# Coefficients, gelu and diagonals of an expert pair ahead of the dense work of odd ticks

## The reference, cut to what matters

```python
def peer_ffn(h, w_q, sub_keys, u_tab, v_tab):
    ...
    expert = i1 * PEER_KEYS + i2
    gate = jax.nn.softmax(best_s, axis=-1)
    u_e = jnp.take(u_tab, expert, axis=0)
    v_e = jnp.take(v_tab, expert, axis=0)
    act = jax.nn.gelu(jnp.einsum('chkd,cd->chk', u_e, xc).astype(jnp.float32))
    return jnp.einsum('chk,chkd->cd', (gate * act).astype(v_e.dtype), v_e)

def reference(...):
    for l in range(DEPTH):
        ...
        x = x + peer_ffn(rmsnorm(x, norm_ffn_g[l]), peer_wq[l], peer_sub_keys[l], peer_u[l], peer_v[l])
    return rmsnorm(x, final_norm_g)
```

## Time and profile before

| | |
|---|---|
| time, median of 3 runs | 1727.95 us (1727.3 to 1729.12) |
| the profiled execution's own time | 1728.54 us |
| its span, first to last instruction | 1726.5 us |
| granted TensorE clock, mean | 0.99 of full |
| bytes moved by DMA | 680.38 MB, 394 GB/s over the span |
| experts' gathers | 512, 536.90 MB |
| busy share | PE 91%, PE weight load 55%, VectorE 70%, ScalarE 35%, GpSimd 34% |

### The profile page before, as it was taken

One profiled execution on the slowest core, in us unless ns is written; L12 is line 12 of the kernel. 1 busy time (PEld: TensorE's weight loads), 2 busy tenths in 40 slices (PEclk: granted clock), 3 DMA queues, 4 the chain that ended last, 5 costly groups with the idle time before them and its releaser, 6 DMA issues.

```text
span 1726.5 us, 19576 instructions
## 1 busy us (share of the span) xinstructions
PE 1579.6 (91%) x6594; PEld 957.9 (55%) x6594; DVE 1212.9 (70%) x3359; ACT 601.0 (35%) x1451; POOL 586.4 (34%) x527
## 2 busy tenths in 40 slices
PE   8999999998999999998999889999999997777776
PEld 7877866545557776644645557644655553322232
DVE  7731689985885767897556477898656677667665
ACT  4133341553344132255232242255323223222222
POOL 0000243443333323344334243344333344433331
PEclk9999999999999999999999999999999999999999
DMA  9637799999999999999999999999999999999996
GB/s 382 243 131 263 291 403 422 415 413 421 421 420 420 422 421 421 420 413 420 421 422 420 421 416 420 421 363 407 422 421 421 421 419 421 421 421 422 422 421 259
DMA packets 94579, 680.38 MB, mean 394 GB/s; under 512 B 10488, under 2 KB 10768, under 8 KB 12304
## 3 DMA queue, kind: packets, MB, share of 16 engines
q0 software_dynamic: 73728, 536.90, 75.2%
q1 hardware_dynamic: 20752, 142.24, 20.4%
HBM read 678.06 MB, written 1.05 MB: 393 GB/s over the span
## 4 chain that ended last, share of the span: by engine, by line
PE 48%; DMA 33%; DVE 11%; ACT 5%; issue 3%; POOL 0%; SPq 0%; DVEq 0%; ACTq 0%
DMA slots<-expert_rows,expert 32%; PE bank L855 21%; PE bank L412 9%; DVE slots L1780 5%; PE bank L590 4%; PE bank L843 3%; PE bank L840 3%; ACT diag L1308 1%; PE bank L457 1%; DMA ring<-w_blocks 1%; PE bank L475 1%; DVE sg L1347 1%; PE bank L678 1%; PE bank L490 1%; ACT L1321 1%
## 5 line engine op out<-in xcount | busy, mean ns | idle before, releaser
L855 PE MATMUL bank<-slots,diag 128*128 128x512 f32 x1916 | 904.0, 608 | 127.8 <-ACT diag L1308 125.4
L967 POOL DMA_INDIRECT slots<-expert_rows,expert x512 | 584.5, 1142 | 1115.1 <-PE bank L855 861.6
L1780 DVE CUSTOM_DVE_ANT_0 slots<-slots,htok 128x1024 f32<-128x1024 f32 x512 | 626.1, 1223 | 332.4 <-DMA slots<-expert_rows,expert 322.6
L855 PEld LDWEIGHTS bank<-slots,diag 128*128 128x128 f32 x1916 | 346.7, 192 | 541.1 <-issue 321.3
L1321 ACT ACTIVATE gel<-dot 128x2 f32<-128x2 f32 (+1 forms) x258 | 52.5, 204 | 671.9 <-DVE dot L1780 664.0
L412 PEld LDWEIGHTS bank<-hT,ring 128*128 128x128 f32 x1712 | 208.5, 193 | 50.5 <-issue 44.9
L1308 ACT ACTIVATE diag<-ident,coef 128x128 f32<-128x128 f32 x479 | 168.2, 395 | 186.2 <-DVE coef L1347 179.5
L412 PE MATMUL bank<-hT,ring 128*128 128x128 f32 x1712 | 209.8, 276 | 4.8 <-DMA ring<-w_blocks 3.9
L1347 DVE SCALAR_TENSOR_TENSOR coef<-gel,ginv,gexp 128x2 f32<-128x2 f32 (+1 forms) x258 | 54.6, 212 | 57.6 <-ACT gel L1321 49.2
L1321 ACT ACT_TABLE_LOAD x66 | 84.7, 1283 | 1.2
L1347 DVE SCALAR_TENSOR_TENSOR sg<-pad,prm,sg 128x128 f32<-128x128 f32 x240 | 71.4, 342 | 0.0
(11 more groups left out here) (315 smaller groups left out, 1543.2 us busy)
## 6 DMA issues: line engine op xcount, KB each, us to landing
ring<-w_blocks SPq DMA_DIRECT2D x98, 1024.0 KB
slots<-w_blocks SPq DMA_DIRECT2D x24, 1024.0 KB, 8.0
slots<-expert_rows,expert POOLq DMA_INDIRECT x512
kept<-w_blocks SPq DMA_DIRECT2D x4, 1024.0 KB, 11.4
keys<-w_blocks SPq DMA_DIRECT2D x2, 1024.0 KB, 10.8
prm<-small SPq DMA_DIRECT2D x2, 768.0 KB
x<-x_rows SPq DMA_DIRECT2D x2, 512.0 KB, 11.0
slots<-mem_rows SPq DMA_DIRECT2D x1, 1024.0 KB, 9.8
```

What stands on the lines that cost most here:

```text
L855: last = mm(bank[h][:, :], diag[:, i % DIAGS, :], slots[:, n % SLOTS, D + h * 512:D + (h + 1) * 512], start=m == 0, stop=n == end)
L967: nc.gpsimd.indirect_dma_start(slots[:, n % SLOTS, :], None, experts_d, bass.IndirectOffsetOnAxis(ap=idx[q % 2][:, k:k + 1], axis=0),).the ...
L1780: v.tensor_tensor_reduce(out=slots[:, s, 0:D], in0=slots[:, s, 0:D], in1=htok[:, ph % 2, :], scale=1.0, scalar=0.0, op0=ALU.mult, op1=ALU.add,
```

## The change

In odd ticks that have a pair, ACT now makes gelu first, then waits for the coefficients and makes both diagonals, and only then does the dense pieces of that tick. Nothing of the experts is left at the head of even ticks. VectorE does the route piece ahead of the dense pieces in every tick, and in odd ticks it waits for gelu and makes the coefficients ahead of the dense pieces and of an add of its own. For the last four experts, ACT makes the diagonal in the tick of its gelu. No instruction is added or taken away, and no buffer is changed.

```diff
@@ scalar engine
             for tick in range(LAST):
                 n = tick - G0
-                if 2 <= n <= SINGLE and n % 2 == 0:
-                    eng.wait_ge(coef_ready, n // 2)
-                    for k in (n - 2, n - 1):
+                if 0 <= n < SINGLE and n % 2:
+                    gelu(n - 1, 2)
+                    eng.wait_ge(coef_ready, n // 2 + 1)
+                    for k in (n - 1, n):
                         if TAKER[k] == "tensor":
                             diagonal(k)
-                if SINGLE < n <= NG:
-                    eng.wait_ge(coef_ready, SINGLE // 2 + n - SINGLE)
-                    diagonal(n - 1)
                 go_on(strands, tick)
-                if 0 <= n < SINGLE and n % 2:
-                    gelu(n - 1, 2)
                 if SINGLE <= n < NG:
                     gelu(n, 1)
+                    eng.wait_ge(coef_ready, SINGLE // 2 + n - SINGLE + 1)
+                    diagonal(n)
@@ vector engine
-                go_on(strands, tick)
                 go_on(route, tick)
-                if 2 <= n <= NG and n % 2 == 0 and TAKER[n - 1] == "vector":
-                    add_slot(n - 1)
                 if 0 <= n < SINGLE and n % 2:
                     eng.wait_ge(gelu_ready, n // 2 + 1)
                     coefficients(n - 1, 2)
+                go_on(strands, tick)
+                if 2 <= n <= NG and n % 2 == 0 and TAKER[n - 1] == "vector":
+                    add_slot(n - 1)
```

## The result

| | before | after |
|---|---|---|
| median of the runs | 1727.84 us (6 runs, 1726.03 to 1729.12) | 1735.97 us (6 runs, 1732.67 to 1738.99) |
| ratio, 95% interval | | 1.0048 (1.0037 to 1.0059) |
| profiled execution, its span | 1728.54, 1726.5 us | 1738.99, 1737.0 us |

The change makes the kernel slower by 0.0048 x 1728 = 8.3 us (6.4 to 10.2), where no change was forecast (1728.4), and its median lies just above the range that the forecast gave, 1723.0 to 1735.0. The profiled execution of after is the slowest of its six, 3 us above their median, so its losses sum to more than 8.3.

The account below looks back on a forecast made before the run. DMA engines were taken as the bound. Start -1.0, stage 3 +0.8, stages 1 and 2 +0.3 each made +0.4 us, a profiled 1728.9; with runs' median 0.6 lower, the forecast was 1728.4 us, range 1723.0 to 1735.0.

Parts of the forecast that it names:

- What bounds the kernel: From the first gathers on, DMA engines set the end; full at 421 GB/s, idle 12 us in all, the largest possible gain.
- Part 1: Coefficients ahead of VectorE's dense pieces: slots freed earlier, gaining 1.0 us per VectorE-bound stretch, bounds 0 and 2.5 us.
- Part 2: VectorE's new wait for gelu in odd ticks: 1.8 us lost in stage 3, the same taken for stages 1 and 2.
- +0.3 each: Net loss in us summed for stages 1 and 2, in place of +0.8, as filled slots hide part.
- their engines hardly idled: Reason for the smaller loss in stages 1 and 2: DMA engines idled only 1.3 and 0.9 us there.
- Part 3: ACT's dense pieces behind gelu and diagonals in odd ticks: price 0; 6 us a stage if the cover were gone.
- five gathers ahead: Cover in full DMA stretches: about five gathers issued ahead of the dot, 12 us of work, outlast PE's 6 us loss.
- Part 4: Start, end and rest: first coefficients some 4 us earlier, part of the 240 us gap goes; gain 1.0 us, bounds 0 and 1.9.
- A: Rival, slower: VectorE's new waits count in full in attention ticks of stages 1 to 3; 5.4 us, about 1733.5; chance 0.20.
- The test set for A: In the windows 1120 to 1200 us, DMA idle time exceeds 10 us; near 7 would confirm the forecast.
- B: Rival, faster: earlier release fills DMA gaps in stage 3 (4.8 us) and at the start (1.0); about 1722.5 us; chance 0.20.
- C: Rival, slower: PE's stalls for held-back ACT evacuations aren't covered, 6 us a stage, 18 us in all: 1746 us; chance 0.05.

Follow-up runs that it names:

- VectorE's lateness at `BEGIN` + 81: Kernel before plus a needless 2600-element VectorE reduction (2.85 us), behind the coefficients, in tick `BEGIN` + 81 of each attention stage: 1728.48 us, ratio 0.9999.
- all but the 15 ticks and the start: Changed kernel with the old order up to n = 10 and in ticks `BEGIN` + 33, 37, 41, 45, 47 of stages 1 to 3: 1727.99 us, ratio 1.0008.
- the 15 ticks alone: Kernel before with the new order only in ticks `BEGIN` + 33, 37, 41, 45, 47 of stages 1 to 3: 1733.06 us, ratio 1.0039.
- 2.85 us of pure lateness: Two kernels: before plus a needless 2600-element VectorE reduction in tick `BEGIN` + 41 per attention stage, behind coefficients (1732.85 us) or ahead of dense pieces (1733.38 us).
- half of it: Kernel before plus a needless 1300-element VectorE reduction (1.50 us), behind the coefficients of tick `BEGIN` + 41 in each attention stage: 1731.49 us, ratio 1.0014.

## Why the prediction was wrong

**What bounds the kernel**: right. The loss is idle time of the DMA engines (11.8 us in the windows for 10.5 of span), most of it in the three attention stretches that the prediction named. That full stretches hide what happens in them holds for VectorE's lateness at `BEGIN` + 81, where 2.85 us cost nothing, but not for every stall: 200 to 240 us was full before and lost 1.7 us.

**Part 1**, coefficients ahead: a gain of 1.0 us in each VectorE-bound stretch was taken. No run shows it. With the new order in all but the 15 ticks and the start nothing is gained, and with it in the 15 ticks alone 6.7 us are lost. The rows of the profile behave as the part says (a diagonal 0.2 to 0.3 us behind its coefficients, 1162.36 against 1162.10), but an earlier diagonal is worth nothing if PE then stands at a later instruction in its list.

**Part 2**, the wait for gelu: three of the four waits came near. VectorE waits 1.69 us at tick 397, where 0.75 was the scan's wait, so 0.9 more (forecast 1.1); 1.28 at tick 401 against 0.17, 1.1 more (forecast 1.6); 0.84 at tick 407 against 1.92, 1.1 less (forecast 0.9 less). But at tick 405, where the prediction had "gelu in time", it waits 1.78 us:

```profile
1176.48 0.25 DVE L1345 SCALAR_TENSOR_TENSOR coef<-gel,ginv,gexp 128x2 f32<-128x2 f32 x1 [1.78 <-ACT gel L1321]
1182.33 0.22 DVE L1345 SCALAR_TENSOR_TENSOR coef<-gel,ginv,gexp 128x2 f32<-128x2 f32 x1 [0.84 <-ACT gel L1321]
```

In sum 2.7 us for stage 3, where 1.8 was said. The wait at 405 comes back from PE: ACT's attention functions ahead of that gelu waited 2.19 us for products of PE that stood behind the late transposes. In the kernel of the fifteen ticks, where PE's stall was shorter, tick 405 has no such wait. The total over the kernel went from 49.2 to 54.5 us:

```profile
DVE coef L1345 <- ACT gel L1321: 54.5, 73, 5.0
```

**The step that failed is the one in the sum** that turned this lateness into time: "+0.3 each" in stages 1 and 2, "part is hidden by filled slots", and 1.0 us set against it. In tick + 41 there is hardly such a cover: 2.85 us of pure lateness cost 2.2 us a stage and half of it 0.8; and the gain of Part 1 that was set against it, 1.0 us a stage, no run shows. The prediction counted how many slots stood filled ahead of VectorE's dot; what the DMA engines need is empty slots, and these are made by PE's adds. PE works its list in order, so the adds stand behind line 508 or behind their own diagonal, whichever is late. In stages 1 and 2 I took "their engines hardly idled" for a cover; it meant that they had more to lose (4.8 and 2.7 us in the windows). A second term stood at nothing without a word: PE's clock. Behind the stall it fell to the lower level in all three stages, and that kept GpSimd waiting 3.2 us longer in stage 3 than at the full clock.

**Part 3**, evacuations behind gelu and diagonals: price 0, "PE needs an odd tick's evacuation in the very next tick only in the memory attention". Wrong in the start: at tick 107 PE waits for the scores' evacuation, 4.28 us against 1.17. ACT's order alone costs 5.0 us (2.9 to 7.1). Its cover in full stretches, "five gathers ahead", held in after, where they stay at 421 GB/s, but not with ACT's order alone: there 2.59 us of waiting for an evacuation at 509.17 left 1.7 us of gaps. In after PE comes to this place otherwise; it waits 5.66 us at 503.62 for VectorE's `htok` and loses nothing. Why the same order loses there in one kernel and not in the other isn't shown; the price of 0 was luck in part.

**Part 4**, the start: first coefficients at 204.54 (forecast 205.5, before 209.46), so the cause was right and the gain of 1.0 wasn't: the windows from 200 to 260 lose 1.4 us against before. The gap that the gain was to be taken from is mostly chance: kernels whose start is untouched read 396 to 416 GB/s from 240 to 260 us, so 0.2 to 1.2 us idle, where the profiled execution of before had 1.9. How much of the start's loss reaches the end stays open (0.7 us by medians, within the uncertainty).

**Rivals.** A is what happened: new waits that count in full in the attention ticks. Its chance (0.20) was too low and its place right; its price, 5.4 us, is near the 6.7 us (4.5 to 8.8) of the 15 ticks. What is left of the 8.3 us, 1.6, is less than the intervals tell from nothing; the start is where the windows would put it. The test set for A, over 10 us idle in 1120 to 1200, reads 80 x 53/421 = 10.1 us. B gained nothing: earlier release fills no gap where PE is late for another reason. C's stalls occur, in after covered, with ACT's order alone in part not.

Two points stay open. The two engines' halves cost 12.1 us apart and 8.3 together; the intervals combined are as wide as that difference (3.9 us), so there may be nothing to explain. And the loss isn't divided between PE's wait itself and the lower clock that follows it: the first is shown to bring the loss, the second only to lengthen the stall.

## What to carry to other kernels

Before a wait is moved ahead of other work in an in-order queue, follow that other work to its consumer. If the consumer is the engine whose later instructions free the buffers, the delay reaches the transfers, even where the queue's own engine isn't the bound. "The slots ahead are filled" covers a delay of the reader, not a delay of the one that empties them; a needless operation of known length, put in at one place at a time, prices both in one run. Removing one such wait (line 508) brought up the next (line 514), with half of the loss left, so a count of one wait is not its price. And work put in to fill a wait must be measured: mine outlasted the wait by 2.3 us and so hid what it was to show.

## What was not expected of the hardware

TensorE's granted clock fell to its lower level (windows of 0.50, the 1.2 GHz level) behind single waits of PE of 1.9 to 4.3 us: in all three stages of after and of both kernels with 2.85 us of lateness, here and there in others. A wait of that length doesn't settle it. Behind 2.02 us at the transposes of stage 3 it fell in the kernel with the new order in tick `BEGIN` + 41 alone and stayed at 1.00 in the profiled execution of the fifteen ticks. At the lower level a group of four 512-column products took 3.33 us against 1.98. Needless products kept the clock at 1.00, but took 5.52 us. In the same place of stage 3 the way from the transposes to GpSimd's next gather took 7.63 us at the lower level and 4.39 and 4.45 at full speed: where the DMA engines lack empty slots, a slow PE makes one short wait a long one.
